# Turns 0 to 6 of a mixer: the exponential of attention unit 1 is issued before the split of the na-gate weights

## The reference, cut to what matters

```
xr, kx, vx, gx, qx, mrx, mnx = jnp.split(xn @ w_in[l], list(IN_SPLITS), axis=-1)
y_rnn_x = h_x * jax.nn.gelu(gx)
y_na_x = neighborhood_attention(rope_2d(qx, row_pos, col_pos), qx, rope_2d(kx, row_pos, col_pos),
                                vx, kc, vc, na_rpb[l])
merged = sigmoid(g_rnn) * (y_rnn @ w_rnn_out) + sigmoid(g_na) * (y_na @ w_na_out)
```

## Time and profile before

| | |
|---|---|
| time, median of 3 runs | 2226.51 us (2225.71 to 2227.54) |
| profiled execution: its own time, its span | 2224.97 us, 2223.2 us |
| busy in the span | PE 96%, PEld 81%, DVE 63%, ACT 43%, POOL 12% |
| turns with the changed order | 7 of 8 |

### The profile page before, as it was taken

The page is one execution under the profiler, slowest core; times in us unless marked ns, Lnnn a source line. Parts: engine busy times, 40 slices in busy tenths (PEclk is TensorE's granted clock), DMA queues, the critical chain, the costliest instruction groups (busy, mean ns, idle before and its releaser), DMA issues.

```text
span 2223.2 us, 27769 instructions
## 1 busy us (share of the span) xinstructions
PE 2133.4 (96%) x10978; PEld 1810.8 (81%) x10978; DVE 1406.1 (63%) x2572; ACT 949.8 (43%) x1467; POOL 270.1 (12%) x204
## 2 busy tenths in 40 slices
PE   5999999999999999999988999989999999999999
PEld 1888888988889888898877888868888888888887
DVE  6688597785976859858589556666553244424542
ACT  3466665666656666666557210013221122202210
POOL 0031222112212113022130100000000000000000
PEclk9999999999999999999999999989999999999999
DMA  8411212012120111111103744421221111111112
GB/s 314 116 53 41 67 41 77 29 39 69 39 79 10 58 60 48 53 37 54 54 20 112 258 152 145 148 96 57 76 67 53 42 53 52 48 57 48 48 57 95
DMA packets 68659, 167.95 MB, mean 76 GB/s; under 512 B 22705, under 2 KB 28209, under 8 KB 68401
## 3 DMA queue, kind: packets, MB, share of 16 engines
q1 hardware_dynamic: 47520, 145.20, 19.7%
q0 software_dynamic: 4608, 16.78, 2.2%
q10 hardware_dynamic: 16400, 4.19, 0.9%
HBM read 145.17 MB, written 25.17 MB: 77 GB/s over the span
## 4 chain that ended last, share of the span: by engine, by line
PE 80%; DVE 10%; ACT 4%; issue 1%; DMA 1%; POOLq 0%; SPq 0%; ACTq 0%; DVEq 0%
PE banks L48 18%; PE banks L50 18%; PE banks L49 18%; PE banks L976 4%; PE banks L847 4%; PE banks L849 4%; PE banks L848 4%; PE banks L880 3%; DVE probT_low L1451 2%; PE banks L938 1%; DVE prob L1443 1%; PE banks L1945 1%; PE banks L920 1%; DVE prob L1439 1%; PE banks L958 1%
## 5 line engine op out<-in xcount | busy, mean ns | idle before, releaser
L48 PE MATMUL banks<-yh,wh 128*128 128x512 f32 x904 | 351.8, 389 | 1.1 <-DVE wl L2005 1.1
L49 PE MATMUL banks<-yl,wh 128*128 128x512 f32 x904 | 351.7, 389 | 0.0
L50 PE MATMUL banks<-yh,wl 128*128 128x512 f32 x904 | 351.7, 389 | 0.0
L48 PE MATMUL banks<-qh,xnh 128*128 128x384 f32 (+1 forms) x640 | 223.3, 349 | 0.3 <-PEq L211 0.3
L847 PE MATMUL banks<-xnh,wh 128*128 128x512 f32 (+1 forms) x536 | 212.3, 396 | 3.8 <-ACT stage L1078 3.6
L50 PE MATMUL banks<-qh,xnl 128*128 128x384 f32 (+1 forms) x640 | 207.5, 324 | 0.0
L49 PE MATMUL banks<-ql,xnh 128*128 128x384 f32 (+1 forms) x640 | 207.4, 324 | 0.0
L848 PE MATMUL banks<-xnl,wh 128*128 128x512 f32 (+1 forms) x536 | 204.7, 382 | 0.0
L849 PE MATMUL banks<-xnh,wl 128*128 128x512 f32 (+1 forms) x536 | 204.7, 382 | 0.0
L48 PEld LDWEIGHTS banks<-yh,wh 128*128 128x128 f32 x904 | 169.7, 188 | 36.6 <-DVE wl L2005 1.5
L49 PEld LDWEIGHTS banks<-yl,wh 128*128 128x128 f32 x904 | 169.7, 188 | 35.3
(11 more groups left out here) (288 smaller groups left out, 4651.6 us busy)
## 6 DMA issues: line engine op xcount, KB each, us to landing
raw<-w_ff SPq DMA_DIRECT2D x68, 512.0 KB, 3.6
raw<-w_fm SPq DMA_DIRECT2D x32, 512.0 KB, 6.9
raw<-w_qkv SPq DMA_DIRECT2D x24, 512.0 KB, 3.8
raw<-w_mix SPq DMA_DIRECT2D x24, 512.0 KB, 4.6
bias<-bias_d SPq DMA_DIRECT2D x16, 448.0 KB, 5.9
wm<-w_modk SPq DMA_DIRECT2D x8, 768.0 KB, 9.7
raw<-w_modT SPq DMA_DIRECT2D x12, 512.0 KB, 3.7
row_c<-w_modT SPq DMA_DIRECT2D x12, 512.0 KB, 3.7
```

What stands on the lines that cost most here:

```text
L48: pe.matmul(out, w_hi(k), x_hi(k), start=(k == 0), stop=False)
L49: pe.matmul(out, w_hi(k), x_lo(k), start=False, stop=False)
L50: last = pe.matmul(out, w_lo(k), x_hi(k), start=False, stop=(k == chunks - 1))
```

## The change

In every turn but the last, `soft(i, 1)`, the exponential of unit 1 with its read-out, is issued directly behind `tr_high(i, JOBS_B)`, whose last copies are those of the rotated queries, and in front of the cast of the MN weights. Its old place, behind `probT_high(i, 0)` in the loop, falls away. Nothing is computed differently, and the other engines' lists stay as they are.

```
                 if last:
                     branch(i, LAST_MN + 1, 3, False, F_ps)
                 else:
+                    soft(i, 1)
                     split_hi(MN, raw_count(MN, i))
                     branch(i, F_MR + 1, 1, first)
                 for u in range(ATT):
                     if u % 2 == 1 and u >= 3:
                         bottoms(i, (u - 3) // 2)
                     probT_high(i, u)
-                    if u + 1 < ATT:
+                    if u + 1 < ATT and (last or u > 0):
                         soft(i, u + 1)
```

## The result

The changed kernel takes 2237.85 us (median of 6 runs, 2233.29 to 2239.75) against 2226.11 us (2222.26 to 2227.54) before, a ratio of 1.0052 with a 95% interval of 1.0039 to 1.0065. It is 11.7 us slower, where the forecast was 2229.4 us in a range of 2226.0 to 2232.0. The profiled execution spans 2236.4 us, 13.2 us more than before.

A forecast was written before the change was run, and what follows sets the result against it. TensorE, busy for 96% of the span, was taken as the bound, with VectorE's low half ending its wait; 7 turns x 0.42 us = 2.9 us on the median 2226.51 gave 2229.4 us, range 2226.0 to 2232.0.

The forecast's parts named there:

- the hole: TensorE's wait between scores of unit 2 and transposes of unit 1, turns 0 to 6: 1.85 us growing to 2.27.
- The cast's slack of 0.60 us: Time from the end of ScalarE's MN cast to VectorE's subtraction taking it up, 0.60 us before the change.
- the slot of 0.92 us: ScalarE time the moved exponential takes ahead of the MN cast, 0.92 us, taken from the exponential of unit 0.
- the handover of 0.10 us: Delay from the end of ScalarE's cast to the start of VectorE's subtraction, 0.10 us.
- The sum: 7 turns x 0.42 us of later subtraction on VectorE = 2.9 us, with bounds of 2.7 to 3.9 us.
- the fourth rival: No slack before VectorE's subtraction, 7 x 0.92 = 6.4 us slower, 2232.9 us; or a lower TensorE clock; chance together 0.09.
- another case: VectorE's subtraction start tied to the MN cast, so 7 x 0.92 = 6.4 us pass on; within the joint chance 0.09.
- the exponential as last releaser: Rival: exponential of unit 1 releases TensorE's transposes last; 0.6 us faster, 2225.9 us; chance 0.05.
- The delay was not absorbed: Rival: a later part of the turn, timed independently, swallows the 0.42 us; 2226.5 us; chance 0.12.
- The full slot: All 0.92 us of the exponential on ScalarE reaches VectorE's subtraction: 6.4 us slower, 2232.9 us; joint chance 0.09.
- the forecast's own list of signs: Expected: ScalarE's new order, cast 0.92 us later, VectorE gap about 0.4 us, TensorE hole 2.2 to 2.4 us, turns 0.4 us longer.
- Its list of what would prove it wrong: No VectorE gap, a TensorE hole smaller than 1.85 us, or turns not longer although the hole has grown.

The follow-up runs named there:

- the first run with the long holes filled: Kernel before, plus unneeded TensorE matmuls in the mixer's longest holes: ten in turn 0, eight and twelve in the last turn; 2227.75 us, ratio 1.0013.

## Why the prediction was wrong

**Right, in mechanism and size.** VectorE's low half ends the hole, not the exponential, although the waits of the earlier trace rows name both. The cast's slack of 0.60 us and the slot of 0.92 us (0.93 measured) gave a gap of 0.42 us on VectorE against 0.44 measured, with the handover of 0.10 us (317.56 to 317.66) as taken from the earlier trace rows. The hole was forecast at 2.27 us and is 2.27. A turn without a fall is 0.40 us longer, so the delay passes through. The run with two matmuls in the hole shows the kernel with little more than this: 2228.6 us.

**The step that failed.** The sum had no term for the clock: a fall behind the longer hole was put at nothing. It stands only at the end of the fourth rival, "0.42 us more could in principle cost it", put together with another case at a chance of 0.09 and without a price. The runs show this term as 1.56 us for each fall, six falls in the profiled execution, 9.4 us, three times the term that was worked out. The argument was that the clock held through 1.85 us in seven turns, which says nothing on 2.27. The trace of before showed the mechanism: behind its holes of 3.44 and 3.63 us the matmuls of 512 columns run at 0.63 instead of 0.39 us. The prediction does not set the new hole beside these. It lay between a length that had held and lengths that had not, so 0 to 7 falls were open; at the 1.56 us that the runs showed, that is 0 to 11 us above the 2.9. How many of the seven fall could not have been read from it, and is not explained by the runs either.

**The other rivals.** Of the exponential as last releaser nothing was seen in the changed kernel; it became so only when the copies delayed it. The delay was not absorbed. The full slot did not pass on. Of the forecast's own list of signs, those on ScalarE and VectorE and the length of the hole came. "The mixer's turns longer by that 0.4 us each" did not: only turn 3 was, the turns with a fall were 1.96 us longer. Its list of what would prove it wrong did not have a turn that grows by more than its hole.

## What to carry to other kernels

When an edit lengthens an idle stretch of TensorE, price two things: the delay, and a fall of the clock behind the stretch. Look up in the same trace after which holes the matmuls were slow and after which not; if the new hole lies between, keep both outcomes, each with its price times the number of places. If an edit has to lengthen such a hole, fill it, with useful work if some is ready: here that took back nearly the whole loss. Filling a hole that costs no fall gained nothing measurable here, nor did filling holes where TensorE soon waits for VectorE again. Look first for what sets the time behind the hole.

## What the runs showed of the hardware that was not expected

Within these turns a hole 0.2 us longer made the difference between no fall and many. Holes of 1.80 to 1.86 us brought no fall in 20 turns of three profiles (the kernel before, the one with two matmuls in the hole, and turns 1 to 6 of the first run with the long holes filled); of 2.04, 2.06, 2.09 and 2.27 us they brought one in 4, 5, 6 and 6 of seven turns. Each count is from one profile. But length is not all: turns of one execution whose holes match to 0.02 us differ in it, and holes of 2.92 us (two runs) and 3.13 us brought a fall in only 5, 4 and 3 of seven turns. In the last turn one and the same hole had no fall behind it before (the first matmul takes 0.50 us) and had one in the changed kernel (0.73 us):

```profile
1150.74 0.50 PE L920 MATMUL banks<-kS,qrS 128*128 128x512 f32 x1 [3.03 <-DVE qrS L1410]
```

```profile
1162.91 0.73 PE L920 MATMUL banks<-kS,qrS 128*128 128x512 f32 x1 [3.04 <-DVE qrS L1411]
```

What else decides was not tested.

Three, five and six tiny instructions ahead of a large one on VectorE delayed what came behind by 1.07, 1.07 and 1.28 us, where 0.2 to 0.4 was planned from rows of that kind. With three and with five the large subtraction itself lasted 0.75 to 0.85 us longer; with six it did not, and the six took 1.3 us. The traces show GpSimd's addition on `stage` at work beside them. In the run with five it starts 0.16 us before the subtraction, which ends 1.09 us after it:

```profile
460.23 1.04 POOL L788 TENSOR_TENSOR stage<-stage,one 128x512 f32<-128x512 f32 x1 [1.71 <-ACT stage L1078]
```

In the kernel before, the subtraction starts first (456.97 us), and it is GpSimd's addition that takes 1.97 instead of 1.04 us. With six, the addition starts among the small instructions and ends before the subtraction. So in these turns the two engines' instructions went one after the other, and the one that started second bore the wait. No run took GpSimd's step away to test it.
